# Two layers, a mixer and sixteen experts on one core: the feed-forward's up projections computed by seven block products instead of eight

## The reference

```python
D_FF = 256 * ((8 * D_MODEL // 3 + 255) // 256)      # 2816
def causal_dwconv(x, w):                            # 3 taps over the tokens
    ...
    return sum(xp[:, j:j + s, :] * w[j] for j in range(k_w))

x = layer_norm(DEEPNORM_ALPHA * x + mix, ln1_g, ln1_b)
hid = causal_dwconv(x @ w_up, ffn_conv_w) + ffn_conv_b
gate, val = jnp.split(hid, 2, -1)
ffn = (jax.nn.silu(gate) * val) @ w_down
return layer_norm(DEEPNORM_ALPHA * x + ffn, ln2_g, ln2_b)
```

## Time and profile before

| | |
|---|---|
| median of three runs | 2250.86 us |
| the profiled execution | 2250.78 us |
| its span, first to last instruction | 2248.9 us |
| mean granted TensorE clock | 0.871 |
| busy: TensorE, VectorE, ScalarE, GpSimd | 1783.0, 552.6, 308.4, 32.7 us |
| up projections, layer 0 (from the first pair to the first down product) | 193.3 to 347.1 us |
| the same in layer 1 | 593.3 to 747.2 us |

### The profile page before, as it was taken

The page is one execution under the profiler, slowest core; times in us unless marked ns, Lnnn a source line. Parts: engine busy times, 40 slices in busy tenths (PEclk is TensorE's granted clock), DMA queues, the critical chain, the costliest instruction groups (busy, mean ns, idle before and its releaser), DMA issues.

```text
span 2248.9 us, 29466 instructions
## 1 busy us (share of the span) xinstructions
PE 1783.0 (79%) x12314; PEld 970.6 (43%) x12314; DVE 552.6 (25%) x1290; ACT 308.4 (14%) x742; POOL 32.7 (1%) x42
## 2 busy tenths in 40 slices
PE   8999999999999999987666676666665665766666
PEld 7867885786788566432211221221121121122122
DVE  3444337444433743420100101010010010010101
ACT  2231110223211112410000000000000000000001
POOL 0010000001100000000000000000000000000000
PEclk9999999999999999988777767877777777687888
DMA  8234543633444365399999999999999999999998
GB/s 289 76 113 136 192 176 115 215 110 113 153 157 150 131 225 211 139 391 420 424 424 425 425 425 424 425 424 425 425 425 425 425 424 424 425 425 424 425 425 338
DMA packets 150713, 693.86 MB, mean 309 GB/s; under 512 B 15984, under 2 KB 65968, under 8 KB 97522
## 3 DMA queue, kind: packets, MB, share of 16 engines
q1 hardware_dynamic: 144482, 683.68, 75.6%
q0 software_dynamic: 6016, 9.04, 1.2%
q10 hardware_dynamic: 144, 0.13, 0.0%
HBM read 691.72 MB, written 4.22 MB: 309 GB/s over the span
## 4 chain that ended last, share of the span: by engine, by line
PE 53%; DMA 38%; SPq 4%; DVE 2%; issue 2%; ACT 1%; DVEq 0%; ACTq 0%
DMA arena<-in_w_up 34%; PE bank L626 16%; PE bank L1235 6%; PE bank L652 6%; PE bank L781 6%; PE bank L1254 4%; DMA arena<-in_w_down 4%; SPq L420 3%; PE bank L1079 1%; PE bank L776 1%; PE bank L988 1%; PE bank L1083 1%; PE bank L1008 1%; DVE arena L2080 1%; PE bank L712 1%
## 5 line engine op out<-in xcount | busy, mean ns | idle before, releaser
L1235 PE MATMUL bank<-arena 128*32 128x512 f32 (+1 forms) x3072 | 472.9, 772 | 279.5 <-DMA arena<-in_w_up 247.2
L626 PE MATMUL bank<-arena 128*128 128x256 f32 (+1 forms) x2208 | 382.7, 335 | 4.1 <-DMA arena<-in_w_in 2.7
L1235 PEld LDWEIGHTS bank<-arena 128*32 128x32 f32 x3072 | 112.6, 138 | 629.2 <-DMA arena<-in_w_up 330.9
L626 PEld LDWEIGHTS bank<-arena 128*128 128x128 f32 x2208 | 346.4, 192 | 41.5 <-issue 4.0
L1254 PE MATMUL bank<-arena 128*32 128x256 f32 x2816 | 224.1, 469 | 116.9 <-DMA arena<-in_w_down 108.4
L2080 DVE TENSOR_TENSOR arena<-arena,bank 64x256 f32<-64x256 f32 x96 | 40.1, 418 | 709.9 <-ACT arena L1524 708.2
L1254 PEld LDWEIGHTS bank<-arena 128*32 128x32 f32 x2816 | 95.9, 131 | 239.9 <-DMA arena<-in_w_down 134.6
L781 PE MATMUL bank<-arena 128*128 128x256 f32 x576 | 138.6, 387 | 0.0
L652 PE MATMUL bank<-arena 128*128 128x512 f32 x308 | 132.7, 592 | 0.0
L1524 ACT ACTIVATE arena<-bank 64x512 f32<-64x512 f32 (+1 forms) x48 | 23.2, 550 | 752.1 <-PE bank L1235 752.1
L1914 DVE SCALAR_TENSOR_TENSOR arena<-bank,arena 128x254 f32<-128x254 f32 (+1 forms) x176 | 76.8, 478 | 184.4 <-ACT arena L1450 181.1
(11 more groups left out here) (295 smaller groups left out, 1324.4 us busy)
## 6 DMA issues: line engine op xcount, KB each, us to landing
arena<-in_w_gate SPq DMA_DIRECT2D x127, 1408.0 KB, 20.9
arena<-in_w_up SPq DMA_DIRECT2D x127, 1408.0 KB, 23.9
arena<-in_w_down SPq DMA_DIRECT2D x144, 1024.0 KB, 17.9
arena<-in_w_down SPq DMA_DIRECT2D x32, 1536.0 KB, 14.8
arena<-in_w_up SPq DMA_DIRECT2D x44, 1024.0 KB, 7.7
arena<-in_w_in SPq DMA_DIRECT2D x40, 1024.0 KB, 8.6
arena<-in_w_out SPq DMA_DIRECT2D x12, 1024.0 KB, 6.0
arena<-in_w_down SPq DMA_DIRECT2D x12, 512.0 KB, 4.2
```

Of the source, the lines that this page charges most:

```text
L626: last = mm(ps[bank][:, j * S + lo:j * S + lo + n], w[:, k, c:c + P], xT[:, k, lo:lo + n], start=(k == 0), stop=(k == KT - 1))
L1235: last = mm(ps[b][32 * q:32 * q + 32, 0:n], expert_x[:, k, :], w, start=(k == 0), stop=(k == KT - 1))
```

## The change

**The pairs from number 3 on** (19 of the 22 of a layer) are computed by seven block products. The weights of a pair are a 2x2 matrix of blocks (input channels 0-511 and 512-1023, value and gate), the tokens another one (the same halves of the channels, tokens 0-127 and 128-255). Each of the seven products has four 128x128 weight tiles and 128 columns. Each goes to its own quarter of one of two PSUM banks.

**Sums of the tokens**: four, t1 to t4, made once a layer by VectorE in `mixT`, which is free then. **Sums of the weights**: four instructions for each pair, on GpSimd (`up_sums`), one of them in place in the ring; three buffers take the results, so GpSimd can be three pairs ahead. **Sums of the products**: seven instructions for each pair on VectorE (`up_summed`), whose result, in the form of the old bank, lies in PSUM bank 2 or 3; the convolution reads it there.

**Moves**: the sums for the first two pairs of the down projection go from VectorE to GpSimd, behind its last weights' sums; VectorE begins with the third when GpSimd is done with two. The four copies of bias rows are issued by ScalarE's queue. Buffers of the sums lie in other places, and three semaphores are merged into others, which moves nothing.

The diff, cut to its core:

```diff
-UP_BANKS = (0, 1, 4, 5)
+UP_BANKS = (0, 1, 4)
+PAIR_BANKS = {0: (4, 5), 1: (0, 1)}
+FIRST_PAIR_BANKS = (6, 7)
+BLOCK_BANKS = (3, 2)
+UP_RING = 3
+POOL_PAIRS = 2
+UP_PLACE = {1: (0, 0), 2: (0, 1), 6: (0, 2), 5: (0, 3), 3: (1, 0), 7: (1, 1), 4: (1, 2)}
...
+            def up_sums(l, j):                                       # GpSimd
...
+                pool.wait_ge(sem(f"slot_in{r}"), l * (UNITS // RING * 32 - first) + 32 * (u // RING + 1) - first)
+                if j >= AHEAD + UP_RING:
+                    pool.wait_ge(sem("up_product"), at(l, "up_product", j - UP_RING + 1))
...
+                nc.gpsimd.tensor_tensor(s1, w[:, 0:4, cg], w[:, 4:8, cg], ALU.add)
+                pool.drain()
+                nc.gpsimd.tensor_tensor(s2, s1, w[:, 0:4, cv], ALU.subtract)
+                nc.gpsimd.tensor_tensor(w[:, 0:4, cg], w[:, 0:4, cv], w[:, 0:4, cg], ALU.subtract)
+                pool.drain()
+                nc.gpsimd.tensor_tensor(s4, w[:, 4:8, cv], s2, ALU.subtract)
+                pool.drain().then_inc(sem("up_sums"), 1)
...
+            def feed_forward_sums(l):
+                for j in range(AHEAD, FT):
+                    up_sums(l, j)
+                for i in range(POOL_PAIRS):
+                    down_sums(l, i)
...
                 if l == 0:
-                    pool.wait_ge(sem("bias_out"), 16)
-                    for n in range(4):
-                        pool.wait_ge(sem("up_product"), 4 + 3 * n)
-                        hs = slice(3 * n, 3 * n + 3)
-                        pool.dma_start(scratch[hs, 2 * S:]..., scratch[hs, 0:2 * S]...).then_inc(sem("bias_out"), 16)
+                    pool.wait_ge(sem("rows_used"), ROW_UNITS + 1)
+                    feed_forward_sums(l)
...
+                def up_block_products(j):                            # TensorE
...
+                    for m in (1, 2, 4, 5, 6, 7, 3):
+                        if m == 5:
+                            pe.wait_ge(sem("up_sums"), at(l, "up_sums", j - AHEAD + 1))
+                        left, right = left_right[m]
+                        b, at_ = UP_PLACE[m]
+                        for k in range(4):
+                            last = mm(ps[pair[b]][:, at_ * P:(at_ + 1) * P], left[:, k, :], right[:, k, :], start=(k == 0), stop=(k == 3))
...
+                pe.wait_ge(sem("x1_copied"), at(l, "x1_copied", 5))
                 for j in range(AHEAD, FT):
...
-                    if j >= 4:
-                        pe.wait_ge(sem("up_convolved"), at(l, "up_convolved", j - 3))
-                    up(j).then_inc(sem("up_product"), 1)
+                    if AHEAD < j <= AHEAD + 2:
+                        pe.wait_ge(sem("up_convolved"), at(l, "up_convolved", AHEAD if j == AHEAD + 1 else 2))
+                    elif j > AHEAD + 2:
+                        pe.wait_ge(sem("up_summed"), at(l, "up_summed", j - 2 - AHEAD + 1))
+                    up_block_products(j).then_inc(sem("up_product"), 1)
...
+                    if l == 0 and j in (4, 7, 10, 13):               # ScalarE
+                        hs = slice(j - 4, j - 1)
+                        act.wait_ge(sem("bias_out"), 16)
+                        act.dma_start(scratch[hs, 2 * S:]..., scratch[hs, 0:2 * S]...).then_inc(sem("bias_repeated"), 16)
...
+                w.tensor_sub(t1, b12, b11)                           # VectorE
+                w.tensor_sub(t3, b22, b12)
+                v.drain()
+                w.tensor_sub(t2, b22, t1)
+                v.drain()
+                w.tensor_sub(t4, t2, b21).then_inc(sem("x1_copied"), 1)
...
+                def up_summed(j):
+                    v.wait_ge(sem("up_product"), at(l, "up_product", j + 1))
...
+                    w.tensor_copy(first, block(pair, 1))
+                    v.drain()
+                    w.tensor_tensor(even, first, block(pair, 6), ALU.add)
+                    w.tensor_tensor(to_[:, 0:1, :], first, block(pair, 2), ALU.add)
+                    v.drain()
+                    w.tensor_tensor(odd_, even, block(pair, 5), ALU.add)
+                    w.tensor_tensor(third, even, block(pair, 7), ALU.add)
+                    v.drain()
+                    w.tensor_tensor(to_[:, 1:4:2, :], odd_.broadcast_to([P, 2, P]), block(pair, 3, 2), ALU.add)
+                    w.tensor_tensor(to_[:, 2:3, :], third, block(pair, 4), ALU.subtract).then_inc(sem("up_summed"), 1)
...
-                    if j in (19, 20):
-                        v.drain()
-                        down_sums(j - 19)
-                v.drain()
-                for i in range(2, KP):
+                v.wait_ge(sem("sums_ready"), at(l, "sums_ready", POOL_PAIRS))
+                for i in range(POOL_PAIRS, KP):
                     down_sums(i)
```

More of the change, by code:

```diff
@@ new lines, in down_sums @@
+            def down_sums(l, i):
+                u = U_DOWN + PAIR_AT[i][0]
+                r, first = u % RING, 16 if u % RING == 0 else 0
+                pool.wait_ge(sem(f"slot_in{r}"), l * (UNITS // RING * 32 - first) + 32 * (u // RING + 1) - first)
+                pool.wait_ge(sem("hidden_ready"), at(l, "hidden_ready", KP + i + 1))
+                (b11, b12, b21, b22), (a11, a21, a12, a22), (s1, s2, s4), (t1, t2, t4) = down_blocks(i)
+                nc.gpsimd.tensor_tensor(t1, b12, b11, ALU.subtract)
+                nc.gpsimd.tensor_tensor(s1, a21, a22, ALU.add)
+                pool.drain()
+                nc.gpsimd.tensor_tensor(t2, b22, t1, ALU.subtract)
+                nc.gpsimd.tensor_tensor(s2, s1, a11, ALU.subtract)
+                nc.gpsimd.tensor_tensor(b12, b22, b12, ALU.subtract)
+                nc.gpsimd.tensor_tensor(a21, a11, a21, ALU.subtract)
+                pool.drain()
+                nc.gpsimd.tensor_tensor(t4, t2, b21, ALU.subtract)
+                nc.gpsimd.tensor_tensor(s4, a12, s2, ALU.subtract)
+                pool.drain().then_inc(sem("sums_ready"), 1)
@@ L1456, in _ @@
+                hidden_silu(FT - 1)
                 f(root_table, ln_eps, ACT.Sqrt)
@@ L1926, in _ @@
-                v.drain()
-                for i in range(2, KP):
+                t1, t2, t3, t4 = (x_sums[:, n] for n in range(4))
+                (b11, b12), (b21, b22) = ((xT[:, k:k + 4, 0:P], xT[:, k:k + 4, P:S]) for k in (0, 4))
+                v.drain()
+                v.wait_ge(sem("x1_copied"), at(l, "x1_copied", 4))
+                w.tensor_sub(t1, b12, b11)
[3 more added lines that the diff above has]
+                v.drain()
@@ new lines, in _, with block @@
+                w.tensor_sub(t4, t2, b21).then_inc(sem("x1_copied"), 1)
+                def block(pair, m, n=1):
+                    b, at_ = UP_PLACE[m]
+                    return ps[pair[b]][:, at_ * P:(at_ + n) * P].rearrange("p (x y) -> p x y", y=P)
+                def up_summed(j):
+                    pair = FIRST_PAIR_BANKS if j == AHEAD else PAIR_BANKS[j % 2]
+                    v.wait_ge(sem("up_product"), at(l, "up_product", j + 1))
+                    to_ = ps[BLOCK_BANKS[j % 2]].rearrange("p (x y) -> p x y", y=P)
+                    first, even, odd_, third = (up_blocks[:, n:n + 1, :] for n in range(4))
+                    w.tensor_copy(first, block(pair, 1))
[8 more added lines that the diff above has]
+                    w.tensor_tensor(to_[:, 2:3, :], third, block(pair, 4), ALU.subtract).then_inc(sem("up_summed"), 1)
@@ new lines, in hidden_product @@
+                def hidden_product(j):
+                    v.wait_ge(sem("gate_silu"), at(l, "gate_silu", j + 1))
+                    w.tensor_mul(hidT[:, j, :], ff_conv[:, j % 3, 0, :], ff_conv[:, j % 3, 1, :]).then_inc(sem("hidden_ready"), 1)
+                for j in range(FT):
+                    if j >= AHEAD:
+                        up_summed(j)
+                    if j > AHEAD:
+                        hidden_product(j - 1)
+                    v.wait_ge(sem("up_last_tap"), at(l, "up_last_tap", j + 1))
+                    for s in range(1, FTAPS):
+                        for gv in range(2):
+                            c = (2 - s) * 2 * FT + gv * FT + j
+                            from_ = ps[UP_BANKS[j] if j < AHEAD else BLOCK_BANKS[j % 2]][:, gv * S:(gv + 1) * S - s]
+                            last = w.scalar_tensor_tensor(ff_conv[:, j % 3, gv, s:S], from_, conv_w[:, 48 + c:49 + c], ff_conv[:, j % 3, gv, s:S], ALU.mult, ALU.add)
+                        if s < FTAPS - 1:
+                            v.drain()
+                    last.then_inc(sem("up_convolved"), 1)
+                    v.drain()
+                    if 0 < j <= AHEAD:
+                        hidden_product(j - 1)
```

124 lines of the change are left out of this document (74 added, 50 removed).

## The result

The changed kernel takes 2226.22 us (median of five runs, 2224.99 to 2227.31) against 2250.77 us for the kernel before (2248.83 to 2251.0). The ratio is 0.9888, with a 95% interval from 0.9877 to 0.9899: 1.1% faster. The profiled execution took 2224.99 us with a span of 2223.2.

What follows compares the result with a forecast made beforehand. TensorE's up stage was taken to bound the part of the kernel that changes. From 2250.78 us, less 25.9 saved on TensorE, plus 3.6 of GpSimd lateness, the forecast was 2228.5 us, range 2223 to 2250.

Steps and rivals of the forecast that it cites:

- TensorE's term: Up stage: 56 records a pair take 6.25 us instead of 6.93, saving 12.95 us a layer, 25.9 in all.
- Rival 4: Up products don't become shorter, because 128 columns don't hide a weight load over a whole stage; chance 0.02.
- VectorE's term: Up stage: block sums 2.12 us, cycle 5.10 a pair under TensorE's 6.25; costs nothing, with 1.15 us of cover.
- Rival 3: VectorE sets the up stage's pace; at 6.9 us a pair nothing is saved (2250); within the 0.08 near no change.
- the passage to the down products: First down pair's product 4 waits for the last taps, E + 5.10, and stands at E + 5.15: nothing, no cover.
- X: GpSimd's own time for one pair's weights' sums in the up stage, forecast at 6.6 us against TensorE's 6.25.
- the 3.6 us of delay: GpSimd's sums for the second down pair come 1.8 us late a layer, 3.6 in all.
- Rival 1: GpSimd and VectorE block each other over SBUF operands in up stage and layer norm: 2243 us; chance 0.18 with mixes.
- The sign that I named for it: A gap on VectorE before gate times value that ends with a GpSimd instruction would show the lock.
- Rival 2: GpSimd sets the up stage's pace, TensorE waiting before each pair's fourth block product: 2260.5 us; chance 0.13.
- the forecast's formula: Delay a layer from GpSimd's sums: 16 X + 238.2 - 342.0 us, for X above 6.49.
- ScalarE's issue of the copies: Four copies issued by ScalarE, 1.17 us each on GpSimd before; ScalarE idles 5.61 us before each pair: nothing.

Runs made afterwards that it cites:

- the doses: Changed kernel with one more GpSimd instruction of 128 columns, one of 512, or two of 512, with drains, in each weights' sum: 2227.27, 2247.4, 2297.26 us.
- the late start: Changed kernel with GpSimd beginning a layer's weights' sums only when VectorE's token sums are done: 2226.61 us.
- dose_one: Changed kernel with one more GpSimd instruction of 512 columns and a drain in each weights' sum: 2247.4 us.
- down_sums_on_vector: Changed kernel with the sums for the first two down pairs on VectorE, behind its last gate times value: 2249.85 us.
- copies_on_gpsimd: Changed kernel with layer 0's four copies of bias rows back on GpSimd's queue, between weights' sums: 2272.04 us.

## Why the prediction was right

**TensorE's term was right, and it carries the forecast**: 12.95 us a layer from the pitch of the earlier trace rows, 131.69 - 118.81 = 12.88 measured. Rival 4 falls: 1064 records of 128 columns, each with its weight load, kept 111.7 ns over a whole stage. One remark beside the sum is off: the two pitches don't have the same 5 ns above their columns. Twice 111.6 is 6.6 ns more than 216.6, so the rows give 0.82 ns a column and 6.6 ns a record. Nothing hung on it, since both pitches went into the sum whole.

**VectorE's term was right**: 2.12 us for the block sums (2.13 measured), and a cover of 1.15 (1.22 idle). Rival 3 falls, and the run with the weights' sums there shows what that cover is worth. At the passage to the down products nothing waited; product 4 of pair 0, for which I found no cover, didn't stop TensorE either.

**The mis-sized term is GpSimd's**: "X = 4 x 1.25 + 3 x 0.56 = 6.6 us a pair", and with it the 3.6 us of delay. Its instructions were right (1.28). The gaps were not: 0.56 came from two rows of before with 0.64 and 0.48, while a drain behind 512 columns leaves 0.14, or 0.24 with the semaphore and the wait of the next group. X is 5.58. What the larger gaps of the earlier trace rows were I can't say: the same instruction behind the same drain has 0.65 in layer 0 and 0.14 in layer 1 of the changed kernel, so it isn't the length of the work ahead.

With X the claim that GpSimd is slower than TensorE's 6.25 was wrong, and the 3.6 us of lateness didn't come. Being off by so little is in part luck. The prediction let GpSimd begin "when the mixer's products are done" with three pairs full early, and that holds in layer 0 only: in layer 1 its own DMAs and the drain behind them take the lead away. By the doses, an X of 6.6 would have cost about nothing in layer 0 and about 6 us in layer 1 (an estimate, 19 x 0.3), not 1.8 in each.

Without the 3.6 us the forecast is 2224.9, and the profiled execution took 2224.99; but 1.0 us of that is the luck of the start, while 0.5 was lost in layer 0's up stage (the late start gives it back) and 0.3 and 0.2 behind the two stages. The median of 2226.22 is the fairer number to compare.

**Rival 1 was there but cheap.** Each of its lengthenings exists: gate times value from 0.43 to 1.05, at most 1.40, the layer norm from 1.28 to 1.9, GpSimd's from 1.28 to 1.47, at most 2.06. I priced it as 0.43 us more in each X. It costs 0.19 on GpSimd in most pairs, which with X at 5.58 disappears in GpSimd's wait for a buffer, and the hold on VectorE, 0.62 in most pairs, fits under ScalarE's 1.02. The layer norm in layer 0 cost TensorE 0.32, inside the 0 to 1.7 I had given. The sign that I named for it, a gap ahead of gate times value, didn't appear: the profile shows the hold as a longer instruction.

**Rival 2's mechanism is real and near.** dose_one puts X at 7.00 and 21 us are gone, where the forecast's formula has 16.4. By the doses the gain would be used up at about 7.1 (an estimate), by the formula at 7.30. The range was right to reach there, since no row of before had the instruction. The part that I cost at nothing, ScalarE's issue of the copies, was right as a price and incomplete as a reason: I asked what the issue costs ScalarE, and not what it would cost GpSimd to keep it, which is 46 us, since GpSimd's drains wait for its own transfers.

## What to carry to other kernels

When work goes to an idle engine, work out its time for each unit of the pacing engine, how far ahead its buffers let it run, and where the first use without slack stands; then the cost beyond the threshold is the slope times the excess. Two doses on that engine measure both, and each place where it starts over (here each layer) has a threshold of its own. On GpSimd, work with drains between dependent steps should have no DMAs of GpSimd's own queue among or shortly ahead of its steps. A wait of 8 to 12 us on TensorE cost more than its length here, since it came back at a lower clock, so the price of such a stall has a second term.

## What the runs showed of the hardware

- A GpSimd drain behind a DMA of its own queue waited until about when the transfer had landed. It took 8.14 us and ended 10.0 us after the last issue, whose transfer landed at 9.4; begun 4.5 us later (late_start), it took 3.88 us and ended 10.2 us after the issue; with no DMA ahead it took 0.14. Behind copies of 768 KB it took 11.50 to 14.80 us and ended 14.0 to 17.2 us after issues that landed after 13.8 to 17.0.
- VectorE instructions with both operands in SBUF were lengthened beside GpSimd's arithmetic, 1.28 to 1.90 and 0.43 to 1.05 us; with one operand in PSUM they were not. GpSimd's own instructions went from 1.28 to between 1.46 and 2.06 beside them.
- After 8 us without a matmul TensorE ran 6 us at a mean granted clock of 0.57 in one layer and 0.74 in the other (down_sums_on_vector), and after 10 us without one 4 us at 0.50 (copies_on_gpsimd). Ahead of the waits, and again behind these stretches, it was 1.00.
- GpSimd's float32 instruction with two operands took 1.28 us at 512 columns, 2.35 at 1024 and 0.46 at 128: about 2.1 ns a column and 0.2 us.
- 1064 float32 records of 128 columns, each with its own weight load, followed each other every 111.7 ns on TensorE for 118.81 us.
